# Split products over 272 tokens: operands of 288, 256 and 272 columns in place of three of 272

## The chip, the core and the metric

The kernel runs on one core of one Trainium2 chip. The metric is the device time of one execution in microseconds, as the median of several runs. Before the change it is 2591.55 us (three runs, 2590.3 to 2593.0).

## What is computed

A stack of blocks on 256 tokens with 2048 features, in float32. The first block puts 16 learned tokens (`meta`) ahead of the 256, so its products run over 272 tokens; the later ones run over 256.

```python
h = concatenate([meta, x])                        # 16 + 256 = 272 tokens
u = rms_norm(h, g_norm) @ w_in                    # hgrn2: q, f, i, z, each 2048 wide (products a_in, a_z)
...                                               # gates, chunked state, heads
h = h + (rms_norm(o) * silu(z)) @ w_out           # a_out
k, v, forget = rms_norm(h, g_kv) @ w_kv           # kv, and fl for the 16 forget columns
h = h + fox_mix(h, ...)                           # b_in, b_out: 256 tokens only
x = h[:, 16:]                                     # the 16 tokens are dropped
x = x + mixed(hyena(x), mlstm(x)) @ w_out         # w2, gates, mg, branches, out2
x = x + (silu(g) * u) @ w_down                    # gate_up, down
return rmsnorm(x)
```

## The kernel before, in words

Tokens lie along the free dimension and features along the 128 partitions, so a product is a set of matmuls whose stationary operand is a 128x128 tile of the weights and whose moving operand is a 128-feature tile of the input with all its tokens. To keep float32 accuracy with TensorE's fast float32 type, both are split: `hi` is the value rounded to the fast type, `lo` is the rest. One 128x128 tile of a product is therefore three matmuls into the same PSUM bank, in `passes` (lines 2007 to 2011): `w_hi` with `x_hi` (L2009), `w_hi` with `x_lo` (L2010), `w_lo` with `x_hi` (L2011). Such a set is called a triple here. `columns` (L2065) has the same three lines written out for the stages in which a product is spread between the work of heads (a_z over 272 tokens, b_in over 256): L2081 to L2083. `down_product` (L2126 to L2128) has the weights as moving operand, 512 columns wide.

Weights come in chunks of 128x1024 through a ring of 4 buffers (`raw`). The sync engine issues the transfers in the order of the chunks, each after VectorE is done with the buffer's last content. ScalarE writes `hi` from `raw` (`chunk`, L573, or `prep`, L578), VectorE writes `lo = raw - hi` (L1124, L1131), TensorE takes the chunk once `lo_ready` says so and frees it with `chunk_used`. The order of each engine's instructions is written out by hand: `follow` puts the work that follows a group of results behind the first few chunks of the next group.

`product` (L2013) goes over pairs; a pair has two groups `gg` of four output tiles (`j`), each group in four PSUM banks of its own (banks 0 to 3 or 4 to 7), over 16 input tiles `k`, two for each chunk. So a group is 16 x 4 x 3 = 192 matmuls. VectorE takes the four banks in one instruction: `scaled` (L1141 to 1148) multiplies by the reciprocal root mean square in `small` and releases the bank group with `bank_free`; `residual` (L1157 to 1162) adds to `H`. In a_z, `a_gate_out` (L1397 to 1402) takes one bank for each of 16 tiles. The work of the heads (lines 2150 to 2210 on TensorE, 1344 to 1389 on VectorE) stands between the parts of a_z.

The input's two halves lie in `XH` and `XL`, one after the other. For 272 tokens tile `k` starts at element 48 + 272k, for 256 tokens at 48 + 256k, with tile 0 at 32 (`STEP` is 16, `KICK` is 32, `WIDE` is 48). ScalarE writes the hi part of four tiles at a time (`a_piece`, `a_split`, `hi_part`), VectorE the lo part (`lo_part`, L1193; `first_x_lo`, L1253). For 272 tokens the two halves of a weight chunk in `hi` and `lo` are put 32 elements apart and shifted by 0 or 32 by the ring slot (`halves`, L356); for 256 tokens and in a_z they lie without gaps.

The products over 272 tokens are a_in (6 pairs), a_out (2), kv (4), each 384 matmuls a pair in triples, fl (16 triples) and a_z (256 triples).

## Time and profile before

| | |
|---|---|
| median of the runs | 2591.55 us (2590.3 to 2593.0) |
| span of the profiled execution | 2591.3 us |
| TensorE busy (matmuls) | 2564.5 us, 99% |
| VectorE busy | 1567.0 us, 60% |
| ScalarE busy | 1212.0 us, 47% |
| GpSimd busy | 69.1 us, 3% |
| DMA | 445.34 MB, 172 GB/s |
| granted TensorE clock, mean | 0.998 of full speed |

The profile is one execution. Engines are PE (TensorE's matmuls), PEld (its weight loads), DVE (VectorE), ACT (ScalarE), POOL (GpSimd). L2009 is line 2009 of the kernel. A matmul's duration in the profile is from its start to its modelled end and overlaps the next one, so the rate of TensorE is read from the distance between starts. The kernel goes, by time: a_in up to about 300 us, a_z with the heads up to 475 us, a_out up to 588 us, kv up to 756 us, fl up to 762 us, then the stages over 256 tokens, and from 2340 us down.

### The profile page before, as it was taken

What the parts mean: (1) busy time and instruction counts of PE and PEld (TensorE: products, weight loads), DVE (VectorE), ACT (ScalarE), POOL (GpSimd) and SP (SyncE); (2) the same over time, 40 slices, a digit from 0 to 9 for tenths busy, and PEclk for the clock granted to TensorE, in tenths of its full rate; (3) what the DMA queues carried; (4) which work ended last, traced back from release to release, by engine and by line L of the source; (5) the groups of instructions that cost most, each with busy time, mean ns of one, the idle gap of its engine ahead of it and who ended that gap; (6) DMA issues with size and microseconds to landing.
All of it is one profiled execution on the core that took longest, in us unless ns stands there. A gap on an engine that the chain in (4) does not pass through costs nothing.

```text
span 2591.3 us, 51017 instructions
## 1 busy us (share of the span) xinstructions
PE 2564.5 (99%) x20256; PEld 2475.2 (96%) x20256; DVE 1567.0 (60%) x1934; ACT 1212.0 (47%) x1432; POOL 69.1 (3%) x64
## 2 busy tenths in 40 slices
PE   9999999999999999999999999999999999999998
PEld 9999999999999999999999998789999999998887
DVE  6445677665456566577765556886655555555444
ACT  5344457543347765443445444334544444443343
POOL 0000022000000000000000000310000000000000
PEclk9999999999999999999999999999999999999999
DMA  6554532455554434655555654236565656566554
GB/s 230 179 175 166 165 112 90 141 173 184 174 173 167 139 123 147 195 196 192 190 193 179 203 194 131 82 107 202 184 199 190 193 193 192 190 193 207 191 187 154
DMA packets 122484, 445.34 MB, mean 172 GB/s; under 512 B 13787, under 2 KB 14070, under 8 KB 122225
## 3 DMA queue, kind: packets, MB, share of 16 engines
q1 hardware_dynamic: 121104, 438.75, 51.6%
q0 software_dynamic: 1248, 4.75, 0.5%
q8 instruction: 94, 1.54, 0.2%
q14 instruction: 38, 0.30, 0.0%
HBM read 441.35 MB, written 2.10 MB: 171 GB/s over the span
## 4 chain that ended last, share of the span: by engine, by line
PE 94%; DVE 3%; ACT 1%; issue 1%; DMA 0%; SPq 0%; DVEq 0%; ACTq 0%
PE PS L2011 23%; PE PS L2009 23%; PE PS L2010 23%; PE PS L2127 3%; PE PS L2126 3%; PE PS L2128 3%; PE PS L2081 3%; PE PS L2083 3%; PE PS L2082 3%; DVE lo L1131 1%; PE PS L2263 1%; PE PS L2454 1%; PE PS L2187 0%; PE PS L2203 0%; PE PS L2533 0%
## 5 line engine op out<-in xcount | busy, mean ns | idle before, releaser
L2009 PE MATMUL PS<-XH,hi 128*128 128x256 f32 (+1 forms) x5152 | 1448.1, 281 | 5.7 <-DVE lo L1124 2.2
L2011 PE MATMUL PS<-XH,lo 128*128 128x256 f32 (+1 forms) x5152 | 1444.3, 280 | 0.0
L2010 PE MATMUL PS<-XL,hi 128*128 128x256 f32 (+1 forms) x5152 | 1439.7, 279 | 0.0
L1124 DVE TENSOR_TENSOR lo<-raw,hi 128x1024 fp32r<-128x1024 f32 x703 | 851.8, 1223 | 757.0 <-ACT hi L573 753.7
L573 ACT ACTIVATE hi<-raw 128x1024 fp32r<-128x1024 f32 x703 | 739.9, 1059 | 949.9 <-PE PS L2011 800.1
L2009 PEld LDWEIGHTS PS<-XH,hi 128*128 128x128 f32 x5152 | 968.7, 188 | 9.0 <-DVE lo L1124 2.7
L2010 PEld LDWEIGHTS PS<-XL,hi 128*128 128x128 f32 x5152 | 971.0, 188 | 1.6 <-issue 1.4
L2011 PEld LDWEIGHTS PS<-XH,lo 128*128 128x128 f32 x5152 | 968.5, 188 | 0.0
L2081 PE MATMUL PS<-XH,hi 128*128 128x256 f32 (+1 forms) x768 | 225.8, 294 | 0.3 <-DVE XL L1196 0.3
L2083 PE MATMUL PS<-XH,lo 128*128 128x256 f32 (+1 forms) x768 | 216.8, 282 | 0.0
L1131 DVE TENSOR_TENSOR lo<-raw,hi 128x1024 fp32r<-128x1024 f32 x124 | 160.2, 1309 | 93.4 <-ACT hi L578 92.3
L2082 PE MATMUL PS<-XL,hi 128*128 128x256 f32 (+1 forms) x768 | 216.7, 282 | 0.0
L578 ACT ACTIVATE hi<-raw 128x1024 fp32r<-128x1024 f32 x124 | 129.0, 1051 | 106.7 <-PE PS L2011 75.6
L2081 PEld LDWEIGHTS PS<-XH,hi 128*128 128x128 f32 x768 | 145.2, 189 | 2.4 <-issue 1.4
L2082 PEld LDWEIGHTS PS<-XL,hi 128*128 128x128 f32 x768 | 145.4, 189 | 1.0
L2083 PEld LDWEIGHTS PS<-XH,lo 128*128 128x128 f32 x768 | 145.3, 189 | 0.0
L2126 PE MATMUL PS<-hi,GH 128*128 128x512 f32 x352 | 137.3, 390 | 0.0
L2127 PE MATMUL PS<-hi,GL 128*128 128x512 f32 x352 | 137.0, 389 | 0.0
L2128 PE MATMUL PS<-lo,GH 128*128 128x512 f32 x352 | 137.0, 389 | 0.0
L2128 PEld LDWEIGHTS PS<-lo,GH 128*128 128x128 f32 x352 | 66.1, 188 | 13.8
L2126 PEld LDWEIGHTS PS<-hi,GH 128*128 128x128 f32 x352 | 66.1, 188 | 13.7
L2127 PEld LDWEIGHTS PS<-hi,GL 128*128 128x128 f32 x352 | 66.1, 188 | 13.5
(357 smaller groups left out, 1557.8 us busy)
## 6 DMA issues: line engine op xcount, KB each, us to landing
raw<-stream SPq DMA_DIRECT2D x827, 512.0 KB, 4.2
out<-f_y SPq DMA_DIRECT2D x4, 512.0 KB, 3.1
H<-h_in SPq DMA_DIRECT2D x3, 544.0 KB, 6.7
w_t<-w POOLq DMA_DIRECT2D x2, 512.0 KB, 4.0
y_win<-windows POOLq DMA_DIRECT2D x2, 512.0 KB, 5.3
f_gain<-gain_f POOLq DMA_DIRECT2D x1, 1024.0 KB, 7.4
H<-h_in SPq DMA_DIRECT2D x2, 272.0 KB, 4.2
raw<-stream SPq DMA_DIRECT2D x2, 256.0 KB, 4.1
```

The costliest lines, as they stand in the source:

```text
L573: act.activation(halves(hi, s, q.tokens, q.shift), raw_halves(s), ACT.Copy).then_inc(hi_ready, 1)
L1124: dve.tensor_tensor(halves(lo, s, q.tokens, q.shift), raw_halves(s), halves(hi, s, q.tokens, q.shift).bitcast(F32), ALU.subtract)\
L1131: dve.tensor_tensor(halves(lo, k % RING, tokens_of(k)), raw_halves(k % RING), halves(hi, k % RING, tokens_of(k)).bitcast(F32), ALU.subtrac ...
L2009: pe.matmul(PS[:, bank, 0:n], w_hi, x_hi, start=start, stop=False)
L2010: pe.matmul(PS[:, bank, 0:n], w_hi, x_lo, start=False, stop=False)
L2011: return pe.matmul(PS[:, bank, 0:n], w_lo, x_hi, start=False, stop=stop)
L2081: pe.matmul(dst, hi[s][:, col], x_hi, start=k == 0, stop=False)
L2082: pe.matmul(dst, hi[s][:, col], x_lo, start=False, stop=False)
L2083: ins = pe.matmul(dst, lo[s][:, col], x_hi, start=False, stop=k == NT - 1)
L2126: pe.matmul(dst, x_hi, w_hi, start=False, stop=False)
L2127: pe.matmul(dst, x_lo, w_hi, start=False, stop=False)
L2128: ins = pe.matmul(dst, x_hi, w_lo, start=False, stop=k == FT - 1)
```

## The change

Only the products over 272 tokens change, and the layout that they need.

- The rest (`lo` part) of the first 16 tokens no longer lies at the head of the tile in `XL`. It is written behind the 272 rounded columns in `XH`, so that a tile of `XH` has 288 columns: 272 rounded ones and 16 rests. `XL` keeps the rests of the other 256 tokens alone.
- The triple becomes: `w_hi` with 288 columns of `XH` (the last 16 land in PSUM columns 272 to 287 of the bank), `w_hi` with 256 columns of `XL` (into PSUM columns 16 to 271), `w_lo` with 272 columns of `XH`.
- VectorE has to add PSUM columns 272 to 287 to the first 16: in `scaled` and `a_gate_out` with two more instructions (`meta_added`: multiply into a small buffer, add), in `residual` with one, for fl with two. The buffer's reuse is guarded by a wait for the other bank group's release, or for the gate before.
- Tiles of `XH` for 272 tokens have a pitch of 320 elements (`PITCH`), with tile 0 at 32 and the others at 48 + 320k, and tiles of `XL` have the place that the 256-token products use. Weight halves lie without gaps everywhere. The extra instructions that write the 16 rests stand in `lo_part` and `first_x_lo`; the hi part of the first piece is written in two instructions.
- `XH` grows and `XL` shrinks; some buffers of the later stages are moved in memory.

```diff
-        x_hi_flat = sb(ctx, "XH", [P, NT * T + 4 * STEP], F32R)
-        x_lo_flat = sb(ctx, "XL", [P, NT * T + 4 * STEP], F32R)
+        x_hi_flat = sb(ctx, "XH", [P, 2 * STEP + KICK + NT * PITCH], F32R)
+        x_lo_flat = sb(ctx, "XL", [P, 2 * STEP + KICK + NT * SEQ], F32R)
...
-            if tokens != T:
-                return buf[s][:, shift:shift + CHUNK].rearrange("p (h n) -> p h n", h=2)
-            at = 2 * STEP * (s % 2)
-            return buf[s][:, at:at + CHUNK + 2 * STEP].rearrange("p (h n) -> p h n", h=2)[:, :, 0:CHUNK // 2]
+        def halves(buf, s, shift=0):
+
+            return buf[s][:, shift:shift + CHUNK].rearrange("p (h n) -> p h n", h=2)
...
-            at = WIDE + k * T if n == T else KICK + (STEP + k * SEQ if k else 0)
+            at = KICK + (STEP + k * (SEQ if n == SEQ else PITCH) if k else 0)
             return flat[:, at:at + n]
...
+            def meta_added(n, dst, rest):
+
+                own(dve.tensor_tensor(meta_t[:, 0:n, :], rest, small[:, 1, 0:META].unsqueeze(1).to_broadcast([P, n, META]),
+                                      ALU.mult))
+                return dve.tensor_tensor(dst, dst, meta_t[:, 0:n, :], ALU.add)
+
             def scaled(q, dst, p_first):
...
+                    if q.tokens == T:
+                        own_last(ins)
+                        dve.wait_ge(bank_free[1 - gg], p + (q.use0[1 - gg] + 1 + gg))
+                        ins = meta_added(GROUP, at[:, :, 0:META], PS[:, 4 * gg:4 * gg + GROUP, T:T + META])
+                    ins.then_inc(bank_free[gg], 1)
...
+                if n == T:
+                    for part, tiles in x_parts(hi_flat, q, T + META):
+                        dve.tensor_tensor(part[:, :, T:], src[:, tiles, 0:META], part[:, :, 0:META].bitcast(F32), ALU.subtract)
+                for (dst, tiles), (part, _) in zip(x_parts(lo_flat, q, SEQ), x_parts(hi_flat, q, n)):
+                    ins = dve.tensor_tensor(dst, src[:, tiles, n - SEQ:], part[:, :, n - SEQ:].bitcast(F32), ALU.subtract)
...
-            def passes(bank, n, w_hi, w_lo, x_hi, x_lo, start, stop):
-
-                pe.matmul(PS[:, bank, 0:n], w_hi, x_hi, start=start, stop=False)
-                pe.matmul(PS[:, bank, 0:n], w_hi, x_lo, start=False, stop=False)
-                return pe.matmul(PS[:, bank, 0:n], w_lo, x_hi, start=False, stop=stop)
+            def passes(bank, col0, n, w_hi, w_lo, k, start, stop, xh=x_hi_flat, xl=x_lo_flat):
+
+
+
+                own = col0 + n - SEQ
+                wide = n + (META if n == T else 0)
+                pe.matmul(PS[:, bank, col0:col0 + wide], w_hi, x_tile(xh, k, wide), start=start, stop=False)
+                pe.matmul(PS[:, bank, own:col0 + n], w_hi, x_tile(xl, k, SEQ), start=False, stop=False)
+                return pe.matmul(PS[:, bank, col0:col0 + n], w_lo, x_tile(xh, k, n), start=False, stop=stop)
```

## Rows read from the trace of the kernel before

**Rows 1.** The page: busy time of the engines, granted clock, chain by engine.

```profile
PE 2564.5 (99%) x20256; PEld 2475.2 (96%) x20256; DVE 1567.0 (60%) x1934; ACT 1212.0 (47%) x1432; POOL 69.1 (3%) x64
...
PEclk9999999999999999999999999999999999999999
...
PE 94%; DVE 3%; ACT 1%; issue 1%; DMA 0%; SPq 0%; DVEq 0%; ACTq 0%
```

**Rows 2.** What PE waited for, largest row: us in total, times, longest.

```profile
PE PS L2009 <- DVE lo L1124: 2.2, 2, 1.8
```

**Rows 3.** Groups by line and form: count, then busy us, mean ns, idle before.

```profile
L2009 PE MATMUL PS<-XH,hi 128*128 128x256 f32 x3600 | 1000.4, 278 | 2.8 <-DVE MG L1863 1.9 <-DVEq L1701 0.6 <-DVE BZ L1522 0.4
...
L2009 PE MATMUL PS<-XH,hi 128*128 128x272 f32 x1552 | 447.6, 288 | 2.8 <-DVE lo L1124 2.2 <-DVE XL L1254 0.6
...
L2081 PE MATMUL PS<-XH,hi 128*128 128x272 f32 x256 | 79.0, 309 | 0.0
```

**Rows 4.** Timeline of PE in a_in: start us, us; 11 matmuls between.

```profile
100.13 0.29 PE L2009 MATMUL PS<-XH,hi 128*128 128x272 f32 x1
...
101.62 0.29 PE L2009 MATMUL PS<-XH,hi 128*128 128x272 f32 x1
```

**Rows 5.** Timeline of PE in gate_up, 256 columns; 11 matmuls between.

```profile
1884.83 0.28 PE L2010 MATMUL PS<-XL,hi 128*128 128x256 f32 x1
...
1886.19 0.28 PE L2010 MATMUL PS<-XL,hi 128*128 128x256 f32 x1
```

**Rows 6.** Timeline of PE in down, 512 columns; 11 matmuls between.

```profile
2349.91 0.39 PE L2126 MATMUL PS<-hi,GH 128*128 128x512 f32 x1
...
2352.63 0.39 PE L2126 MATMUL PS<-hi,GH 128*128 128x512 f32 x1
```

**Rows 7.** Timeline of PE in w2, 256 columns, slower stretch; 11 between.

```profile
1130.72 0.28 PE L2009 MATMUL PS<-XH,hi 128*128 128x256 f32 x1
...
1132.14 0.28 PE L2009 MATMUL PS<-XH,hi 128*128 128x256 f32 x1
```

**Rows 8.** Timeline of PE in a_z, 272 columns; 46 matmuls between.

```profile
313.96 0.29 PE L2082 MATMUL PS<-XL,hi 128*128 128x272 f32 x1
...
319.87 0.27 PE L2165 MATMUL PS<-cst,AV 128*16 128x128 f32 x1
```

**Rows 9.** Two lines of VectorE by source: ns min/median/max, first and last start.

```profile
L1350 DVE TENSOR_TENSOR a_W<-AB x16: 157/166/171, 308.6 to 451.3; 128x16 f32<-128x16 f32 x16
L1387 DVE COPY a_SS<-PS x16: 279/291/292, 329.4 to 469.9; 128x128 f32<-128x128 f32 x16
```

**Rows 10.** Timelines of DVE and PE around the first result of a_in.

```profile
41.74 1.29 DVE L1146 TENSOR_TENSOR AQ<-PS,small 128x1088 f32<-128x1088 f32 x1 [0.15 <-DVE a_VT L1307]
...
45.16 3.50 DVE L1124 TENSOR_TENSOR lo<-raw,hi 128x1024 fp32r<-128x1024 f32 x3 [2.13 <-ACT hi L573]
...
46.44 0.40 PE L2009 MATMUL PS<-XH,hi 128*128 128x272 f32 x1 [0.40 <-DVE lo L1124]
```

**Rows 11.** Timelines of DVE and PE from the last result of a_in on.

```profile
299.77 1.29 DVE L1146 TENSOR_TENSOR AV<-PS,small 128x1088 f32<-128x1088 f32 x1 [0.60 <-PE PS L2011]
...
310.41 0.44 DVE L1356 TENSOR_TENSOR a_W<-AQ,a_W 128x272 f32<-128x272 f32 x1 [1.68 <-ACT AB L698]
...
311.71 0.77 DVE L1402 TENSOR_TENSOR AZ<-PS,small 128x272 f32<-128x272 f32 x2
...
318.13 2.82 DVE L1131 TENSOR_TENSOR lo<-raw,hi 128x1024 fp32r<-128x1024 f32 x2 [2.55 <-ACT hi L578]
...
322.07 0.49 PE L2171 MATMUL PS<-cst,a_W 128*16 128x128 f32 x3 [1.71 <-DVE a_KT L1368]
```

**Rows 12.** Timeline of DVE in a running head.

```profile
344.97 0.42 DVE L1366 COPY a_KT<-PS 64x256 f32<-64x256 f32 x1 [1.72 <-PE PS L2171]
```

**Rows 13.** Timeline of DVE at the end of kv.

```profile
761.24 1.28 DVE L1146 TENSOR_TENSOR BV<-PS,small 128x1088 f32<-128x1088 f32 x1
763.16 2.43 DVE L1196 TENSOR_TENSOR XL<-BN,XH 128x256 fp32r<-128x256 f32 x3 [0.63 <-ACT XH L557]
```

More of the change, by code:

```diff
@@ L572, in chunk @@
                 act.wait_ge(chunk_used, q.index(p, gg, c) + 1)
-                act.activation(halves(hi, s, q.tokens, q.shift), raw_halves(s), ACT.Copy).then_inc(hi_ready, 1)
+                act.activation(halves(hi, s, q.shift), raw_halves(s), ACT.Copy).then_inc(hi_ready, 1)
             def prep(k):
@@ L1161, in after @@
                     dst = H[:, p * 8 + 4 * gg:p * 8 + 4 * gg + 4, T - q.tokens:T]
-                    dve.tensor_tensor(dst, dst, bank_group(gg, q.tokens), ALU.add).then_inc(bank_free[gg], 1)
+                    ins = dve.tensor_tensor(dst, dst, bank_group(gg, q.tokens), ALU.add)
+                    if q.tokens == T:
+                        own(ins)
+                        ins = dve.tensor_tensor(dst[:, :, 0:META], dst[:, :, 0:META],
+                                                PS[:, 4 * gg:4 * gg + GROUP, T:T + META], ALU.add)
+                    ins.then_inc(bank_free[gg], 1)
                     dve.wait_ge(bank_free[gg], p + (q.use0[gg] + 2))
@@ L1193, in lo_part @@
             def lo_part(lo_flat, hi_flat, q, n, src):
-                for (dst, tiles), (part, _) in zip(x_parts(lo_flat, q, n), x_parts(hi_flat, q, n)):
-                    ins = dve.tensor_tensor(dst, src[:, tiles, :], part.bitcast(F32), ALU.subtract)
+                if n == T:
[3 more added lines that the diff above has]
+                    ins = dve.tensor_tensor(dst, src[:, tiles, n - SEQ:], part[:, :, n - SEQ:].bitcast(F32), ALU.subtract)
                 return ins
@@ L1401, in a_gate_out @@
                     dve.wait_ge(S("a_vt"), tile - 3)
-                dve.tensor_tensor(a_gate(tile), PS[:, 1 + 2 * (tile % 2), 0:T], small[:, 1, 0:T], ALU.mult)\
-                    .then_inc(S("a_zout"), 1)
+                bank = 1 + 2 * (tile % 2)
+                own_last(dve.tensor_tensor(a_gate(tile), PS[:, bank, 0:T], small[:, 1, 0:T], ALU.mult))
+                if tile:
+                    dve.wait_ge(S("a_zout"), tile)
+                else:
+                    dve.wait_ge(bank_free[1], q.use0[1] + 1)
+                meta_added(1, a_gate(tile)[:, 0:META].unsqueeze(1), PS[:, bank:bank + 1, T:T + META]).then_inc(S("a_zout"), 1)
             def a_finish(g):
@@ L1492, in b_input @@
                 own(dve.tensor_tensor(F_row[:, 0, :], PS[0:HEADS, 0, 0:T], small[0:HEADS, 1, :], ALU.mult))
+                own(dve.tensor_tensor(F_row[:, 1, 0:META], PS[0:HEADS, 0, T:T + META], small[0:HEADS, 1, 0:META], ALU.mult))
+                own(dve.tensor_tensor(F_row[:, 0, 0:META], F_row[:, 0, 0:META], F_row[:, 1, 0:META], ALU.add))
                 dve.sem_inc(bank_free[0], 1)
@@ L2078, in columns @@
                     col = slice(128 * kk, 128 * kk + 128)
-                    dst = PS[:, bank, col0:col0 + q.tokens]
-                    x_hi, x_lo = x_tile(x_hi_flat, k, q.tokens), x_tile(x_lo_flat, k, q.tokens)
-                    pe.matmul(dst, hi[s][:, col], x_hi, start=k == 0, stop=False)
-                    pe.matmul(dst, hi[s][:, col], x_lo, start=False, stop=False)
-                    ins = pe.matmul(dst, lo[s][:, col], x_hi, start=False, stop=k == NT - 1)
+                    ins = passes(bank, col0, q.tokens, hi[s][:, col], lo[s][:, col], k, k == 0, k == NT - 1)
                 if kks.stop == 8:
```

85 lines of the change are left out of this document (42 added, 43 removed).

## Prediction

> **What bounds the kernel now.** I read the page's shares and its chain of work first [rows 1]: TensorE is busy for 2564.5 of 2591.3 us, and 94% of the chain that ended last is matmuls, nearly all at the three lines of the split product. So the time is the number of matmuls times the spacing between them, plus some 27 us in which TensorE stands idle; the waits of TensorE [rows 2] show no single stall longer than 1.8 us. The profiled span (2591.3 us) is 0.25 us below the median of the runs (2591.55 us), so what is worked out on the span can be set against the median.
>
> The second look is at the forms [rows 3]. There are 1552 triples of 272 columns at lines 2009 to 2011 (the products a_in, a_out, kv and the small fl), 256 more at lines 2081 to 2083 (a_z), together 1808; the later stages have triples of 256 columns, and down has 512 columns. The mean of one matmul in these rows is a latency with overlap, no price: the spacing of starts is, and it has to be taken from the timeline.
>
> Third look, the timeline. I count from a start to the twelfth start behind it. 272 columns in a product: 1.49 us, 124.1 ns each [rows 4]. 256 columns: 1.36 us, 113.3 ns [rows 5]. 512 columns: 2.72 us, 226.7 ns [rows 6]. The last two are in exact proportion, 0.4427 ns for a column. In that proportion 272 columns would take 120.4 ns, so each pays 3.7 ns more than its columns. That is not fixed to the width: in another stretch the same 256-column form runs at 1.42 us for twelve, 118.3 ns each, without a wait [rows 7], 5 ns above its columns; so there is a second way for these streams to run, and 256 can be in either. In a_z, where the weights lie unpadded and the input tile changes with every triple, 272 columns take 5.91 us for 47, 125.7 ns [rows 8]. The granted clock reads nine tenths or more in every slice [rows 1], so the engine stays at its 2.4 GHz level and the clock explains none of it.
>
> **The change, part by part.** *Columns.* Before, a triple streams 272 + 272 + 272 = 816 columns; after, 288 + 256 + 272 = 816. No column and no matmul is saved. A gain can come only from the 3.7 ns and 5.3 ns above proportion.
>
> *The triple in the products.* Price before: 3 x 124.1 = 372.3 ns. After, matmul by matmul: the 256-column one is taken at 113.3 ns [rows 5], with 118.3 ns as its upper end [rows 7]. The 272-column one stays at 124.1 ns. 288 columns in one matmul are nowhere in the trace; its columns cost 288 x 0.4427 = 127.5 ns, which is the lower end. For the upper end I let the excess grow with the columns above 256, twice 3.7, which gives 134.9 ns. I take 127.5 + 3.7 = 131.2, since 272 is the nearest width and 512, much wider, pays no excess at all [rows 6]. Sum 113.3 + 131.2 + 124.1 = 368.6 ns, 3.7 less than before. Times 1552: -5.7 us.
>
> *The triple in a_z.* Before 3 x 125.7 = 377.1 ns. The input tiles now start at a pitch of 320, a multiple of 64 elements, as the 256-column products have with their pitch of 256, and weights lie unpadded in both. I price it like the products, 368.6 ns: 8.5 x 256 = -2.2 us. If only the product's old pace is reached it is 4.8 x 256 = -1.2 us; if nothing, 0.
>
> A rule of the Trainium skill speaks against the change. In "TensorE: Matmul & The Clock Gate", section "Back-to-back issue gap", the warm spacing is the columns divided by 2.4 GHz plus 2.5 ns, which gives 109.2 ns for 256 and 115.8 ns for 272. The trace doesn't agree on the size. By that rule both triples cost the same 347.5 ns, and the change would bring nothing from TensorE. That outcome is the second rival below, worked out there from rows.
>
> *VectorE work added.* Each group result (scaled, 20 of them) gets two small operations on 4 x 16 elements, with a wait for the main one; each a_out group one; each of the 16 gates of a_z two; fl two; each input piece of 272 tokens one or two more for the rests. The nearest row is an operation on 128x16 at 167 ns, and a copy of 128x128 out of PSUM at 291 ns bounds it from above [rows 9]. I take 0.22 us for each dependent one, 0.45 us for a pair (0.3 to 0.6). In all some 90 operations, about 20 us on an engine that is busy for 1567 us; the main subtraction of the rests becomes 16 columns in 272 shorter. What counts is where TensorE waits for VectorE:
> - The first group result of a_in, at 41.7 us, is followed by ScalarE's Silu and weight rounding, VectorE's subtraction at 45.2 us, and a TensorE stall of 0.40 us at 46.4 us [rows 10]. Nothing covers the pair there: +0.45 us.
> - The last group result of a_in at 299.8 us is followed by the forget gates, scans, weight subtraction and the first two gates at 311.7 us, up to TensorE's stall of 1.7 us at 322.1 us [rows 11]. One pair, and two gates with a pair each: up to 1.3 us, of which a part falls into VectorE's own waits for ScalarE (1.7 and 2.6 us on the way). I take +0.9 us.
> - In the running heads the gate stands just ahead of the key copy, which at 345.0 us comes after 1.72 us of VectorE's waiting for TensorE; that hides the pair [rows 12]. Without that cover it would be 0.45 us x 12.
> - The last kv result at 761.2 us ends 0.63 us before the next subtraction can start, which waits for ScalarE [rows 13]: hidden. With a longer pair, up to 0.3 us.
> - The banks: TensorE comes back to a bank group one group later, 192 matmuls or 23.8 us, and the result now takes 1.75 instead of 1.3 us: hidden. The new wait for the other group's bank_free is for a result already written; behind it on VectorE only stand the small operations and the next subtractions, and it isn't due to last.
> - The two operations for fl and the extra cut of the first input piece: 0.1 us, between 0 and 0.4.
>
> Sum of these +1.4 us (0 to 3). DMA, and the masks and sums that are moved to other places in memory, cost nothing: the same number of transfers at the same places in the queues; that they would land on data in use is excluded by their old waits.
>
> **Sum.** -5.7 - 2.2 + 1.4 = -6.5 us: 2591.55 - 6.5 = 2585.0 us, 0.25% faster. Its own range from the terms' bounds is 2581 to 2589 us.
>
> **The rivals.**
> 1. *The excess vanishes in the whole triple.* For it: 256 and 512 run at exact proportion, and a 256-column matmul in every triple, with starts that always lie equally, may bring the stream back each time into the pattern of [rows 5]. Against it: [rows 7] shows that equal starts alone don't do that. Triple 816 x 0.4427 = 361.3 ns: -11.0 x 1552 = -17.1 us, -15.8 x 256 = -4.0 us, +1.4 us: 2571.8 us. In between, the excess of one more matmul gone, lies 2578 us.
> 2. *Only columns and their excess count.* The excess goes with the columns above 256: 16 + 16 + 16 before, 32 + 0 + 16 after, the same 48. Or it is an average over the places in a cycle that the streams run through either way. For it: the 124.1 ns doesn't change over the whole stage. Then products don't gain, a_z gains 0 to 1.2 us, VectorE's additions cost 1.4 us: 2591.8 to 2593 us, 2592 taken. (By the page's rule the same.)
> 3. *Slower.* The wide operand upsets the one behind it: the 256-column matmul runs at 118.3 ns [rows 7], and the 288-column one at 134.9 ns. Triple 118.3 + 134.9 + 124.1 = 377.3 ns, +5.0 x 1552 = +7.8 us, a_z 0, VectorE +1.4 us: 2600.8 us. It decides once a triple is above 372.3 ns + 2.5 ns. For it: the slow pattern of 256 columns follows a disturbance and then holds. Against it: 512-column matmuls stay clean next to their loads.
> That the change doesn't do what it says is small: the second operand has no other columns to stream.
>
> **Chances.** Forecast 0.32; rival 1 with its middle 0.30; rival 2 0.25; rival 3 0.13. 0.2%, 5.2 us, is about what a measurement of this kernel can tell from no change, so faster ends at 2586.4 us and slower begins at 2596.7 us. Of the forecast two thirds lie below 2586.4. Faster 0.22 + 0.30 = 0.52, same 0.10 + 0.25 = 0.35, slower 0.13. The range holds the forecast and rival 2, reaches to 2571 for nearly all of rival 1, and stops at 2597, short of rival 3 at its full price.
>
> **What would show it.** In the timeline of the changed kernel, in the stretch from 60 to 290 us: twelve matmuls in 1.474 us (four triples of 368.6 ns), and in them a step of 113.3 ns behind the 256-column start. 1.445 us would be rival 1, 1.49 us rival 2, 1.51 us rival 3. a_z should show the same triples as the products. The stall of 0.40 us near 46 us should read 0.8 to 0.9 us, the one near 322 us should be longer; the heads between should have none. The stages behind 770 us should have the same lengths as before. The prediction is wrong if the triples of 288, 256 and 272 have another sum, or if new waits for VectorE stand in the heads.

## The result, and the profile after

| | before | after |
|---|---|---|
| median, 20 runs each on one chip | 2591.47 us | 2596.28 us |
| ratio, with its 95% interval | | 1.0016 (1.0010 to 1.0022) |
| span of the profiled execution | 2591.3 us | 2594.2 us |
| device time of that execution | 2593.1 us | 2596.0 us |

The changed kernel is 4.8 us slower by the two medians and 4.1 us by the ratio (2.6 to 5.7 us), where 6.5 us less were forecast. So it moved the other way, clear of the noise. 2596.3 us lies at the upper end of the range, and with 0.16% just inside "within 0.2%". The last row corrects a sentence of the prediction: the device time is the span and 1.7 to 1.9 us more, in every run of a whole kernel here. So the profiled execution of before was no median one: it took 1.6 us more than the median, the one of after 0.3 us less. That is why the traces stand 2.9 us apart and the medians 4.8 us.

The page after, the same lines as [rows 1]:

```profile
PE 2565.2 (99%) x20256; PEld 2475.9 (95%) x20256; DVE 1583.2 (61%) x2029; ACT 1212.2 (47%) x1434; POOL 66.3 (3%) x64
...
PE 93%; DVE 4%; ACT 1%; issue 1%; DMA 0%; SPq 0%; DVEq 0%; ACTq 0%
```

The number of matmuls is the same; VectorE has 95 instructions and 16.2 us more, and one hundredth of the chain has passed from TensorE to it. All triples are at L2038 to L2040 now. Timeline of TensorE in a_in, columns as in [rows 4]: first four starts in a row, then the second matmul of a group, of its fourth input tile and of its last one, 36 and 144 matmuls apart.

```profile
102.43 0.30 PE L2038 MATMUL PS<-XH,hi 128*128 128x288 f32 x1
102.56 0.28 PE L2039 MATMUL PS<-XL,hi 128*128 128x256 f32 x1
102.68 0.29 PE L2040 MATMUL PS<-XH,lo 128*128 128x272 f32 x1
102.80 0.30 PE L2038 MATMUL PS<-XH,hi 128*128 128x288 f32 x1
```

```profile
85.35 0.28 PE L2039 MATMUL PS<-XL,hi 128*128 128x256 f32 x1
...
89.87 0.28 PE L2039 MATMUL PS<-XL,hi 128*128 128x256 f32 x1
...
107.79 0.28 PE L2039 MATMUL PS<-XL,hi 128*128 128x256 f32 x1
```

107.79 - 89.87 = 17.92 us for 48 triples, 373.3 ns each. The three tiles ahead of them took 4.52 us for 12 triples, 376.7 ns. Over whole groups that is 374.0 ns. In the same way before has 372.1 ns in every tile. Within a triple the steps average 133.1 ns behind the 288-column start, 116.6 ns behind the 256-column one and 124.3 ns behind the 272-column one. In a_z, from the second matmul of the first stretch to the head's work 47 matmuls later (the pair that answers to [rows 8]):

```profile
317.12 0.28 PE L2039 MATMUL PS<-XL,hi 128*128 128x256 f32 x1
...
322.72 0.28 PE L2039 MATMUL PS<-XL,hi 128*128 128x256 f32 x1
...
322.96 0.49 PE L2187 MATMUL PS<-cst,AV 128*16 128x128 f32 x3
```

5.84 us where before had 5.91. The widths differ here, so 5.84 us can't simply be divided by 47: the stretch holds 15 whole triples and then a 256-column and a 272-column step, and one of the dear 288-column steps is missing. The 15 whole triples, from 317.12 to 322.72 us, take 5.60 us, 373.3 ns each by these rounded rows. Over all of a_z at full clock, with the steps of each operand averaged, a triple takes 374.6 ns after 377.6. So a_z gained 3.0 ns, and the products lost 1.9 ns.

From the rates and the stalls below the whole difference can be added up: 1.9 x 1552 = +2.9 us, -3.0 x 256 = -0.8 us, and +2.3 us of stalls, together +4.4 us.

Where TensorE waits for VectorE, timeline of TensorE after, waits in brackets (they answer to [rows 10, 11]):

```profile
47.37 0.40 PE L2038 MATMUL PS<-XH,hi 128*128 128x288 f32 x1 [0.75 <-DVE lo L1120]
...
315.01 0.50 PE L2193 MATMUL PS<-cst,a_W 128*16 128x128 f32 x3 [0.83 <-POOL AB L511]
316.91 0.38 PE L2038 MATMUL PS<-XH,hi 128*128 128x288 f32 x1 [0.61 <-DVE lo L1127]
...
325.21 0.49 PE L2193 MATMUL PS<-cst,a_W 128*16 128x128 f32 x3 [1.76 <-DVE a_KT L1386]
...
334.42 0.68 PE L2220 MATMUL PS<-a_AM,a_VT 128*128 128x16 f32 x4 [0.46 <-DVE a_SS L1407]
...
432.01 0.72 PE L2232 MATMUL PS<-AF,cst 128*128 128x272 f32 x2 [1.01 <-ACT AQ L701]
```

Before, the same places read 0.40, 0.29, nothing, 1.71, nothing and 0.68 us. The four that grew and the two that are new come to 2.3 us. What VectorE does there (its timeline, the first group result and the first two gates):

```profile
42.27 1.29 DVE L1149 TENSOR_TENSOR AQ<-PS,small 128x1088 f32<-128x1088 f32 x1 [0.15 <-DVE a_VT L1325]
43.48 0.21 DVE L1139 TENSOR_TENSOR h_dif<-PS,small 128x64 f32<-128x64 f32 x1
43.73 0.23 DVE L1141 TENSOR_TENSOR AQ<-AQ,h_dif 128x64 f32<-128x64 f32 x1
...
314.26 0.43 DVE L1421 TENSOR_TENSOR AZ<-PS,small 128x272 f32<-128x272 f32 x1
314.61 0.16 DVE L1139 TENSOR_TENSOR h_dif<-PS,small 128x16 f32<-128x16 f32 x1
314.80 0.18 DVE L1141 TENSOR_TENSOR AZ<-AZ,h_dif 128x16 f32<-128x16 f32 x1
314.91 0.43 DVE L1421 TENSOR_TENSOR AZ<-PS,small 128x272 f32<-128x272 f32 x1
```

A pair at a group result ends 0.40 us after its main operation (43.96 against 43.56). At a gate the next one starts 0.65 us behind the last; before, two took 0.77 us together, 0.38 us each.

One thing in the two traces is not the change. Granted clock by stretch: behind the 1.7 us stall, before has a stretch at half speed, after none. First before, then after (stretch, length, TensorE busy, its granted clock, DMA share, GB/s):

```profile
324.00:326.00 2.00, 2.00 (x10) 0.50 0.64 201
326.00:328.00 2.00, 2.00 (x14) 0.75 0.55 217
```

```profile
326.00:328.00 2.00, 1.77 (x15) 1.00 0.78 248
328.00:332.00 4.00, 4.00 (x35) 1.00 0.42 135
```

At 0.50 of full speed, the 1.2 GHz level, the matmuls start 227 ns apart. Before's 24 matmuls from 323.83 us take 4.38 us to the last start, after's from 326.84 us 2.96 us: the change is credited 1.4 us there by chance. Of the runs below, three have such a drop too: the changed kernel without tile 0 set back (0.57 from 318 to 322 us, behind its stall at 317.8 us), the run at a pitch of 288 (behind its stall of 1.72 us at 320.5 us) and the run cut to 256 columns (from 294.7 us on). In the opening, from 12 to 20 us, the clock differs from trace to trace as well. Small differences have to be read from rates and stalls, or from medians, not from two spans.

### The profile page after: what moved, and what is told of

Read it like the earlier page. It is cut to its first block, busy times and chain, and to the rows that moved or that the text cites. A ratio compares the mean times of both kernels' runs of the same rounds, so it can differ in the third digit from the quotient of the medians.

```text
span 2594.2 us, 51114 instructions
## 1 busy us (share of the span) xinstructions
PE 2565.2 (99%) x20256; PEld 2475.9 (95%) x20256; DVE 1583.2 (61%) x2029; ACT 1212.2 (47%) x1434; POOL 66.3 (3%) x64
## 4 chain that ended last, share of the span: by engine, by line
PE 93%; DVE 4%; ACT 1%; issue 1%; DMA 0%; SPq 0%; DVEq 0%; ACTq 0%
PE PS L2038 26%; PE PS L2040 26%; PE PS L2039 25%; PE PS L2150 3%; PE PS L2149 3%; PE PS L2148 3%; DVE lo L1127 1%; PE PS L2285 1%; PE PS L2476 1%; PE PS L2209 0%; PE PS L2225 0%; PE PS L2554 0%; PE PS L2493 0%; PE PS L2220 0%; PE PS L2199 0%
## 5 line engine op out<-in xcount | busy, mean ns | idle before, releaser
L2038 PE MATMUL PS<-XH,hi 128*128 128x256 f32 (+1 forms) x5920 | 1688.5, 285 | 7.0 <-DVE lo L1120 3.2
L2040 PE MATMUL PS<-XH,lo 128*128 128x256 f32 (+1 forms) x5920 | 1657.9, 280 | 0.0
L2039 PE MATMUL PS<-XL,hi 128*128 128x256 f32 x5920 | 1645.2, 278 | 0.0
L2038 PEld LDWEIGHTS PS<-XH,hi 128*128 128x128 f32 x5920 | 1113.8, 188 | 12.3 <-DVE lo L1120 3.6
L2040 PEld LDWEIGHTS PS<-XH,lo 128*128 128x128 f32 x5920 | 1114.3, 188 | 0.0
L554 ACT ACTIVATE GH<-g_p 128x1024 f32 (+3 forms) x12 | 11.8, 990 | 46.9 <-DVE g_p L1986 46.9
L1058 ACT ACTIVATE g_s<-g_s 128x1024 f32<-128x1024 f32 x11 | 11.7, 1061 | 31.1 <-DVE g_s L1981 31.1
L510 POOL TENSOR_TENSOR a_W<-AF,a_W 128x272 f32<-128x272 f32 x16 | 14.1, 883 | 412.3 <-ACT AB L695 412.3
L692 ACT ACTIVATE a_W<-a_W 128x272 f32<-128x272 f32 x16 | 6.8, 427 | 38.1 <-DVE a_W L1368 38.0
L1211 DVE TENSOR_TENSOR GL<-g_p,GH 128x1024 f32 (+3 forms) x12 | 13.5, 1136 | 15.6 <-ACT GH L554 15.6
L2225 PE MATMUL PS<-AB,a_SS 128*128 128x64 f32 x128 | 17.8, 262 | 0.0
```

The source lines that it names most:

```text
L2038: pe.matmul(PS[:, bank, col0:col0 + wide], w_hi, x_tile(xh, k, wide), start=start, stop=False)
L2039: pe.matmul(PS[:, bank, own:col0 + n], w_hi, x_tile(xl, k, SEQ), start=False, stop=False)
L2040: return pe.matmul(PS[:, bank, col0:col0 + n], w_lo, x_tile(xh, k, n), start=False, stop=stop)
```

## The experiments

Two theories stood at the start. *Widths*: a 256-column matmul keeps its clean 113.3 ns only among its like, and 288 columns pay more above proportion than 272. *Places*: the loss comes from where the operands lie, since the change moved them all. The additions of VectorE got a run of their own. In all the rates below I count 144 starts (48 triples, tiles 3 to 15 of a group).

**A bare loop over widths.** The kernel keeps the streams and leaves out the computation. It runs triples of matmuls on constant operands, with the weights and input tiles where the products have them, in 24 sets one after the other. Its `passes`:

```diff
+                            for i, (wb, xb) in enumerate(((hi, x_hi_flat), (hi, x_lo_flat), (lo, x_hi_flat))):
+                                wd = widths[i]
+                                x = (xk + k * pitches[i]) if k else x0
+                                c0 = 16 if (wd == 256 and widths[0] > 256 and i == 1) else 0
+                                pe.matmul(PS[:, 4 * gg + j, c0:c0 + wd], wb[s][:, w], xb[:, x:x + wd], start=False, stop=k == groups[gg] - 1 and i == 2)
```

> The matmul stream by itself. It leaves out the whole computation and sends TensorE 24 sets of matmuls in the order of a product's group (16 input tiles, 4 output tiles, triples of w_hi x XH, w_hi x XL, w_lo x XH, weights in the ring's places) with static operands, each set behind eight 512-column matmuls and a short pause. Only widths, pitch and start of the input tiles and the gaps of the weights differ. Theory A (an excess that goes with the columns by which a width is no multiple of 64): 256 at 113.3 ns, 272 at 124.0, 288/256/272 at 373.9 ns a triple, 288 near 133, 304 at 138 to 141, and 320 back in proportion at 141.7 ns; 320/256/320 would take 396.7 ns. Theory B (the excess comes from where the reads start: input and weights in equal or opposite halves of 64 elements): 272 columns at the new pitch without gaps differ from the old places by over 1 ns, and sets that differ in the start alone (0, 16, 32, 48) differ at 256 columns too. Theory C (a matmul waits for the next weight load, slower the more the moving stream reads): the excess falls with the width, 384 columns at exactly 170.0 ns, and 240 and 128 columns stand at one floor near 112 ns. If 288/256/272 gives 373.9 ns here, the added 1.9 ns a triple of the changed kernel needs no other engine for its cause.

Measured per matmul, three equal widths: 128 columns 111.7 ns, 240: 112.2, 256: 117.8, 272: 124.4, 288: 132.6, 304: 140.0, 320: 145.6, 384: 173.3. A triple of 288, 256 and 272 takes 373.3 ns, 320, 256 and 320 410.0. So 320 columns, a multiple of 64, are not clean (141.7 ns in proportion): theory A, a rule by multiples of 64, falls. Of theory C the floor near 112 ns is there, but 384 columns stand 3.3 ns above its 170.0 ns. 256 never reached 113.3 ns here, though, with any start: something of the kernel's places was not met. `XL` happened to begin 32 elements off `XH`, counted in 64. At these places three of 272 columns take 373.3 ns too, as much as the new triple.

**The loop with XL in its true distance.** Same loop, `XL` a multiple of 64 elements behind `XH`, and sets that move starts.

```diff
-                                x = (xk + k * pitches[i]) if k else x0
+                                x = ((xk + k * pitches[i]) if k else x0) + (xladd if i == 1 else 0)
```

> The matmul stream by itself again (the computation is left out). In the first such run XL lay 32 elements off the real distance from XH modulo 64, and three times 256 columns ran at 117.8 ns and never at 113.3. Here the distance is a multiple of 64 as in both kernels, and sets are added in which XL's start is moved by 16, 32 and 48, the order of the three matmuls is changed, and tile 0 starts elsewhere. Theory B (the state that costs nothing needs equal starts of XH and XL modulo 64): the set of the 256-token products falls to 113.3 ns a matmul, the one with XL moved by 32 stays at 117.8, three times 272 at the old places gives 372.1 ns a triple, and 288/256/272 gives 373.9 ns and depends on XL's start by some ns. Theory D (the free state is a matter of how the stream was started, not of the starts of its operands): 256 stays at 117.8 ns in all sets, with tile 0 at 32 or at 48, and the triples of 816 columns all lie between 373 and 375 ns. If one of the added sets of 288/256/272 lies under 369 ns, it is the setting for a better kernel.

Now three of 256 columns run at 113.3 ns (340.0 ns a triple), but only where tile 0 starts at 32 or 0 and the others at 48. With tile 0 at 48 too, the stream stays at 117.8 ns; timeline of TensorE, tiles 3 to 15 of that set:

```profile
81.08 0.28 PE L350 MATMUL PS<-XH,hi 128*128 128x256 f32 x1
...
98.04 0.28 PE L350 MATMUL PS<-XH,hi 128*128 128x256 f32 x1
```

16.96 us for 144. With all tiles at 0 it is 120.0 ns, and with `XL` moved by 32 elements 117.8 ns. The two paces are those of [rows 5, 7], and in the loop, with the other tiles at 48, the shift of tile 0 decides between them. In the kernel before, the stretch of [rows 7] has that shift too, and the same product runs at 113.3 ns from 1145 us on; what put it into the slower pace stays open. A single wider neighbour is enough: 256, 256 and 272 columns take 357.8 ns, where 113.3 + 113.3 + 124.1 would be 350.7. 288, 256 and 272 columns take 373.3 ns with tile 0 set back or not, and with the three in another order. 3 x 272 at the changed kernel's places takes 370.0 ns: less than the new triple.

**Every place in the real distance.** A third loop with the true gaps between weight halves, and starts that vary.

```diff
-                        at = (32 * (s % 2) + kk * 544) if pad else kk * 512
+                            at = (kk * 512, 32 * (s % 2) + kk * 528, kk * 544)[pad]
```

> The matmul stream by itself (the computation is left out), the sets now with the kernel before's true weight places (half pitch 528, odd slots 32 further) and with the a_z order (one output tile at a time, all input tiles). The last such run gave 353.3 ns for 3 x 256 where the input starts elsewhere than 48 past the weights (modulo 64) or where the first tile isn't set back by 16, 373.3 ns for 288/256/272 and 370.0 ns for 3 x 272 in the changed kernel's places. Theory E (the distance of input and weights modulo 64 sets the pace, and the widths add theirs): the kernel before's places give 372.1 ns in every input tile; 3 x 272 at a pitch of 288 with the weight halves 32 apart, which keeps that distance, gives 370.0 ns like the pitch of 320; with the halves unpadded 373 to 379 ns; other starts (0, 16, 32) 373 to 380 ns. The a_z order gives about 377 ns at the old places, 373.3 ns for 288/256/272 and 370 ns for 3 x 272 at pitch 320. Theory F (only the shape of the triple counts, 370.0 was a chance state of one start): the sets of 3 x 272 scatter between 370 and 379 ns without regard to the distance, and moving tile 0 from 32 to 48 loses the 370.0.

Timelines of TensorE, tiles 3 to 15. First 3 x 256, then before's own triple and places, then 3 x 272 at a pitch of 320, then the new triple, then 3 x 288:

```profile
33.50 0.28 PE L344 MATMUL PS<-XH,hi 128*128 128x256 f32 x1
...
49.82 0.28 PE L344 MATMUL PS<-XH,hi 128*128 128x256 f32 x1
```

```profile
63.67 0.29 PE L344 MATMUL PS<-XH,hi 128*128 128x272 f32 x1
...
81.53 0.29 PE L344 MATMUL PS<-XH,hi 128*128 128x272 f32 x1
```

```profile
196.01 0.28 PE L344 MATMUL PS<-XH,hi 128*128 128x272 f32 x1
...
213.78 0.28 PE L344 MATMUL PS<-XH,hi 128*128 128x272 f32 x1
```

```profile
538.73 0.30 PE L344 MATMUL PS<-XH,hi 128*128 128x288 f32 x1
...
556.65 0.30 PE L344 MATMUL PS<-XH,hi 128*128 128x288 f32 x1
```

```profile
869.28 0.29 PE L344 MATMUL PS<-XH,hi 128*128 128x288 f32 x1
...
888.48 0.29 PE L344 MATMUL PS<-XH,hi 128*128 128x288 f32 x1
```

16.32, 17.86, 17.76, 17.92 and 19.20 us: 340.0, 372.1, 370.0, 373.3 and 400.0 ns a triple. The loop gives both kernels' real rates in the products to a tenth. Moving all tiles of the 370.0 ns case from 48 to 0, 16 or 32 gives 376.0, 380.0 and 380.0 ns, and moving `XL` alone 373.3 ns. In a_z's order of tiles, before's places give 378.3 ns, the new triple 373.6 and 3 x 272 at a pitch of 320 370.0; the kernels have 377.6 and 374.6 ns for the first two, so the loop is within 1 ns there. Widths and places both count, with opposite signs in the changed kernel: places gain 2.1 ns a triple (8 in a_z), widths lose 3.3 ns (3.6 in a_z).

The two aren't independent, though. The second and third loop together have both triples at seven settings of the starts:

| tiles at, `XL` moved by | 3 x 272, ns | 288, 256, 272, ns |
|---|---|---|
| 48, 0 (the changed kernel) | 370.0 | 373.3 |
| 0, 0 | 376.0 | 376.7 |
| 16, 0 | 380.0 | 373.3 |
| 32, 0 | 380.0 | 380.0 |
| 48, 16 | 373.3 | 377.8 |
| 48, 32 | 373.3 | 373.3 |
| 48, 48 | 373.3 | 377.8 |

With the tiles at 16 the new widths are the cheaper ones. Timelines of TensorE, tiles 3 to 15, first 3 x 272 in the third loop, then the new triple in the second, 18.24 and 17.91 us:

```profile
260.79 0.29 PE L344 MATMUL PS<-XH,hi 128*128 128x272 f32 x1
...
279.03 0.29 PE L344 MATMUL PS<-XH,hi 128*128 128x272 f32 x1
```

```profile
561.50 0.29 PE L350 MATMUL PS<-XH,hi 128*128 128x288 f32 x1
...
579.41 0.29 PE L350 MATMUL PS<-XH,hi 128*128 128x288 f32 x1
```

So "widths lose 3.3 ns" is their price at the changed kernel's places; at the others they cost between -6.7 and +4.4 ns. The new widths at before's own places have no run.

**The changed kernel cut to 256 columns.** Behind the first input tile of each group the two matmuls with `XH` are cut to 256 columns, which leaves out the last 16 tokens and the rests of the first 16. If the changed kernel's places or its traffic kept the clean pace away, it would stay away here too.

```diff
+                if n == T and not start:
+                    pe.matmul(PS[:, bank, col0:col0 + SEQ], w_hi, x_tile(xh, k, n)[:, 0:SEQ], start=start, stop=False)
+                    pe.matmul(PS[:, bank, own:col0 + n], w_hi, x_tile(xl, k, SEQ), start=False, stop=False)
+                    return pe.matmul(PS[:, bank, col0:col0 + SEQ], w_lo, x_tile(xh, k, n)[:, 0:SEQ], start=False, stop=stop)
```

> The changed kernel with the 272-token triples cut to 256/256/256 columns behind the first input tile of each group: the last 16 tokens are left out of the two products with XH and the rests of the first 16 are left out. Layout, VectorE work and order stay. It asks whether the new layout can carry the clean pace at all while ScalarE and VectorE write weights. If the loss comes from the widths (288 and 272 never meet the clean state), the triples run at 340.0 ns behind the first tile, the products over 272 tokens lose 33.9 ns for each of 1695 triples, some 57 us, and the kernel takes about 2539 us. If the layout itself (pitch 320, weights without gaps) keeps the stream in the slower state, the triples run at 353.3 ns, and it takes about 2561 us.

2546.74 us, against 2593.0 of before beside it, one execution of each. That is 46.3 us less, between the two expected times. The mean gain is smaller than 33.9 ns a triple, because each group's first tile still takes 380.7 ns, parts of a_z run at up to 353.7 ns, and TensorE now stalls for weights in some places (0.28 us at 220.6, 243.1 and 265.6 us). Timeline of TensorE in the same group of a_in:

```profile
83.61 0.28 PE L2040 MATMUL PS<-XL,hi 128*128 128x256 f32 x1
...
99.92 0.28 PE L2040 MATMUL PS<-XL,hi 128*128 128x256 f32 x1
```

16.3 us for 48 triples, 340 ns. With ScalarE and VectorE writing and the DMA running, the places allow the clean pace right behind the first tiles. So the widths 288 and 272 keep it away. The same rows settle another point. In the new triple the 256-column matmul writes to PSUM columns 16 to 271, not to column 0 on. It still does so here, at 340 ns a triple, so that offset isn't what costs; and in the third loop 272, 288 and 256 columns, all written from column 0, take 373.3 ns too.

**Without the additions.** The changed kernel without VectorE's extra work on results. It leaves out the additions in `scaled`, `residual`, the gates of a_z and fl, so the rests of the first 16 tokens are computed and not added.

```diff
-                    if q.tokens == T:
-                        own_last(ins)
-                        dve.wait_ge(bank_free[1 - gg], p + (q.use0[1 - gg] + 1 + gg))
-                        ins = meta_added(GROUP, at[:, :, 0:META], PS[:, 4 * gg:4 * gg + GROUP, T:T + META])
...
```

> The changed kernel without the additions of PSUM columns 272 to 287: meta_added in scaled and in the gates of a_z, the one in residual, and the two for fl are left out, with the wait for the other bank group, so the rests of the first 16 tokens are computed and not added. If the loss is that of the triples alone (1.9 ns x 1536, and a kick at each group's start), VectorE's additions are worth little: this kernel is 0.5 to 1 us faster than the changed one, some 2595.5 us where the changed one has 2596.3 and the kernel before 2591.5. If the additions carry the loss (rival: chains at the stage ends), it comes out within 1 us of the kernel before. In the profile the stall at 47 us should fall from 0.75 to 0.40 us, and the stall at 315 us from 0.83 to 0.29 us.

2594.87 us, 1.0009 of before (1.0000 to 1.0019). The rate is that of the changed kernel (374.0 ns). Two of the three stalls are back at before's length, the middle one not quite (before 0.29 us):

```profile
46.51 0.40 PE L2023 MATMUL PS<-XH,hi 128*128 128x288 f32 x1 [0.36 <-DVE lo L1120]
...
313.78 0.50 PE L2178 MATMUL PS<-cst,a_W 128*16 128x128 f32 x3 [0.46 <-POOL AB L511]
...
429.31 0.72 PE L2217 MATMUL PS<-AF,cst 128*128 128x272 f32 x2 [0.72 <-ACT AQ L701]
```

0.36, 0.46 and 0.72 us in place of 0.75, 0.83 and 1.01, and those at 316.91 and 334.42 us are gone: 2.1 us. That is more than the 0.5 to 1 us expected. By the ratios the additions cost 0.07%, 1.8 us, but with 2.9 us to either side that alone doesn't show a cost: the stalls do.

**Before's triple at a pitch of 288.** It computes everything. The weight halves lie 32 elements apart in all ring slots. It was meant as a half of the places' gain that fits into memory easily.

```diff
+PITCH = 288
-            at = WIDE + k * T if n == T else KICK + (STEP + k * SEQ if k else 0)
+            at = KICK + (STEP + k * (SEQ if n == SEQ else PITCH) if k else 0)
...
```

> The kernel before with its triple of 272/272/272 and without the additions, in places that fit the memory and keep the distance of input and weights at 48 modulo 64: input tiles at a pitch of 288 with tile 0 at 32, weight halves 32 elements apart in all ring slots. It does the layout part of the change alone. Theory E: triples at 370.0 ns in the products, 2.1 less than before's 372.1, less 11 ns for four triples at each group's first tile: 1536 x 2.1 = 3.2 us less, 24 groups x 44 ns = 1.1 us more, a_z between its old 377 and 373 ns (0 to 1 us less): 2.1 to 3.1 us below the kernel before, and 6 to 8 us below the changed one. Theory F: triples at 372 to 375 ns, no better than the kernel before (0 to +3 us). No stall should be longer than before's, since VectorE has the old work but one more instruction's cut of the first piece.

2592.62 us, 1.0002 (0.9993 to 1.0011). The 370.0 ns that were expected aren't there: the steady triple is 371.7 ns, as in the third loop (371.7), and the first tiles take 373.2 and 376.2 ns, so the mean is 372.1 as before: no gain. Tile 0 set back costs here, and 3 x 272 columns get nothing for it.

**The widths alone, in the whole kernel.** The kernel without the additions, with three times 272 columns again at the same places. Its second operand reads 272 columns of `XL` that belong to other tokens, and the rests of the first 16 tokens aren't read, so it leaves out part of the rests. One start differs: tile 0 of `XL` lies at 48, not at 32.

```diff
+                if n == T:
+                    pe.matmul(PS[:, bank, col0:col0 + n], w_hi, x_tile(xh, k, n), start=start, stop=False)
+                    at = STEP + KICK + ((k - (k % 4 == 3)) if k >= 4 else k // 2) * SEQ
+                    rest = xl[:, at:at + T]
+                    pe.matmul(PS[:, bank, col0:col0 + n], w_hi, rest, start=False, stop=False)
+                    return pe.matmul(PS[:, bank, col0:col0 + n], w_lo, x_tile(xh, k, n), start=False, stop=stop)
...
```

> The changed kernel's places (pitch 320, tile 0 at 32, weight halves without gaps), none of its additions, and 272, 272, 272 columns in a triple again. It leaves out the rests of the values: the second operand of a triple reads 272 columns in XL from a start that is as far from the weights and from XH as in the changed kernel, but their values belong to other tokens, and the first one has no 16 rests. So against the kernel without the additions it differs in widths alone. My theory (the widths 288 and 256 cost more than three of 272 at the same places): triples of 370.0 ns behind the first input tile, about 371 ns on the mean, in a_z too, 3 ns less than 373.97 ns, so 1808 x 3 = 5.4 us less than without the additions: 0.999 of the kernel before (0.998 to 1.000). Rival (the widths don't matter, the loss is the new places): 374 ns again, and 1.001 of the kernel before.

2587.28 us, 0.9982 (0.9973 to 0.9991). Triples of 370.0 ns behind the first tiles, 370.4 on the mean. Timeline of TensorE in a_in (second matmul, fourth tile, last tile):

```profile
83.66 0.29 PE L2028 MATMUL PS<-XL,hi 128*128 128x272 f32 x1
...
88.12 0.29 PE L2028 MATMUL PS<-XL,hi 128*128 128x272 f32 x1
...
105.88 0.29 PE L2028 MATMUL PS<-XL,hi 128*128 128x272 f32 x1
```

Against the run without the additions the widths differ (and that one start), and 1.0009 - 0.9982 = 0.27%, 7.0 us, with 3.4 us to either side. From the rates: (374.0 - 370.4) x 1552 = 5.6 us, and 374.3 - 371.2 ns in a_z, 0.8 us. The widths of the change are its loss.

**Tile 0 like the others.** The same with tile 0 of the 272-token products at 48, and then the whole changed kernel so.

```diff
-            at = KICK + (STEP + k * (SEQ if n == SEQ else PITCH) if k else 0)
+            at = KICK + (STEP + k * (SEQ if n == SEQ else PITCH) if k or meta else 0)
...
```

> As the run with 272, 272, 272 columns at the changed kernel's places, with the same parts left out, but tile 0 of a product over 272 tokens starts at 48 like the others, not at 32. My theory: tile 0 set back costs about 10 ns a triple for its four triples in each group and buys nothing at these widths. Then the triples are 370.0 ns from the first tile on, 24 groups x 40 ns = 1 us less than with it, 0.9985 of the kernel before. Rival (the set-back tile is what brings the stream to its better pace): triples stay at 373 ns or more without it, and the time is longer than with it.

2588.03 us, 0.9983 (0.9974 to 0.9992): 370.0 ns from the first triple on, but no gain that the medians show.

> The changed kernel whole, additions too, but tile 0 of the products over 272 tokens starts at 48 in XH and XL, not at 32. Nothing is left out. My theory: the pace of 373.3 ns is there from the first tile, and 380 and 376.8 ns of the first two input tiles are gone: 1.0 us less than the changed kernel, a ratio of 1.0012 to 1.0014 against the kernel before where the changed kernel had 1.0016. Rival (tile 0 set back is needed at these widths, as it is for 256 columns, where without it a matmul takes 117.8 and not 113.3 ns): the triple is above 373.3 ns all through, up to 377 ns, and the ratio is 1.003 or more.

2594.99 us, 1.0011 (1.0002 to 1.0020). Timeline of TensorE, group's start and fourth tile:

```profile
86.59 0.28 PE L2039 MATMUL PS<-XL,hi 128*128 128x256 f32 x1
...
91.08 0.28 PE L2039 MATMUL PS<-XL,hi 128*128 128x256 f32 x1
```

36 matmuls in 4.49 us after 4.52 us, that is 374.2 ns a triple in place of 376.7 by rounded rows; over nine groups it is 373.3 ns in all tiles. The rates give 1.0 us (373.96 - 373.33, times 1552), the ratios 0.05%, 1.3 us, with intervals that overlap. The set-back tile isn't needed at these widths.

**The places alone, with nothing left out.** It computes everything, as the kernel before does. Both input halves at a pitch of 320 need 4 KB more of each partition than in the changed kernel. They fit if the tail of `XL` shares its room with a buffer of the second block that is written later, and three buffers of the first block lie in `h2_sum` and `h2_dif`.

```diff
+        with ExitStack() as ph:
+            x_lo_flat = sb(ph, "XL", [P, 2 * STEP + KICK + NT * PITCH], F32R)
+        sb(ctx, "XL_256", [P, 2 * STEP + KICK + NT * SEQ], F32R)
...
+            sb(ph, "XL_tail", [P, 960])
             AQ = sb(ph, "AQ", [P, NT, T])
...
+            a_AM = [sb(ph, "a_AM0", [P, T]), h2[:, 0:T]]
...
+            b_PT = [sb(ph, f"b_PT{s}", [P, 640]) for s in range(2)]
             BK = sb(ph, "BK", [P, NT, T])
...
```

> The kernel before with the changed kernel's places alone: three matmuls of 272 columns with all their values, no additions, XH and XL both at a pitch of 320 with tile 0 at 32, weight halves without gaps. The room for the longer XL comes from b_PT, which now lies over its tail in the second block, and from a_AM, gam and dec, which lie in h2_sum and h2_dif in the first. Nothing is left out. My theory (the places are the half of the change that gains, the widths the half that loses): triples of 370.0 ns behind the first input tile, 370.4 on the mean, in a_z 371 after 376.8: 1552 x 1.7 + 256 x 5.8 = 4.1 us less than before, 0.9984 of it (0.9975 to 0.9993). Rival (the 0.9982 with the rests left out came from something that the missing values or XL's shorter tiles bring): triples of 372 ns and a ratio of 1.000.

2588.66 us, 0.9985 (0.9976 to 0.9994): 370.0 ns behind the first tiles, 370.6 on the mean, 371.4 in a_z. The rates give (372.1 - 370.6) x 1552 + (377.6 - 371.4) x 256 = 3.9 us, as the ratio does.

> As the run with 272 columns three times at a pitch of 320 and nothing left out, but tile 0 starts at 48 like the others. My theory: 370.0 ns in every triple of the products from the first on, 24 groups x 40 ns = 1.0 us less than with tile 0 at 32: 0.998 of the kernel before. Rival (tile 0 set back makes no difference between two whole runs): the same ratio within 0.0003, and only the trace shows the 380 ns triples gone.

2587.45 us, 0.9981 (0.9972 to 0.9990), the fastest kernel here that computes everything: 4.6 us less than before. The two can't be told apart by their medians. Timeline of TensorE in the group of a_in (second matmul, fourth tile, last tile):

```profile
84.87 0.28 PE L2013 MATMUL PS<-XL,hi 128*128 128x272 f32 x1
...
89.31 0.28 PE L2013 MATMUL PS<-XL,hi 128*128 128x272 f32 x1
...
107.07 0.28 PE L2013 MATMUL PS<-XL,hi 128*128 128x272 f32 x1
```

4.44 us and 17.76 us, 370.0 ns in both. The rates account for (372.1 - 370.0) x 1552 = 3.3 us in the products, and its a_z for the rest: 370.6 ns a triple after 377.6 (from 313.37 to 319.17 us 47 equal matmuls, 370.2 ns a triple, where [rows 8] has 377.1), 7.0 x 256 = 1.8 us; together 5.1 us.

## Why the prediction was wrong

- *What bounds the kernel.* Right: all of the result is in the spacing of matmuls and in TensorE's stalls for VectorE. The step that set the span beside the median was wrong by 1.8 us, without effect on the forecast. The range "from the terms' bounds", 2581 to 2589 us, doesn't follow from them: with 127.5 ns for 288 columns and no stalls the sum is 2577 us, with 118.3 and 134.9 ns, nothing in a_z and 3 us of stalls it is 2602 us.
- *The triple in the products: the step that failed.* Forecast 113.3 + 131.2 + 124.1 = 368.6 ns, measured 116.6 + 133.1 + 124.3 = 374.0 ns. The difference of 5.4 ns is 8.4 us of 1552 triples, most of the 11.3 us between forecast and result; a_z has 1.4 us of it and the stalls 0.9 us. Two terms failed, by 3.3 and 1.9 ns: the 256-column price was taken from a stage in which every matmul is that wide [rows 5], and the 288-column one was given the excess of its neighbour of 272. The loops have 113.3 ns only where the whole stream is 256 columns wide, with its starts in certain places (240 columns reached it too). It is no price of a matmul: a single one among wider ones took 116.1 ns or more in the loops' steady stretches at the changed kernel's places. The excess above proportion is 5.1 to 5.8 ns at 288, with 3.7 at 272 [rows 4].
- *Columns aren't the price.* Both triples have 816 columns, 361.3 ns by proportion. By the formula of the Trainium skill ("TensorE: Matmul & The Clock Gate", section "Back-to-back issue gap"), which the page gives for a matmul by itself and not for a stream with weight loads, they cost the same. The loop has 370.0 and 373.3 ns for them at the changed kernel's places, and 380.0 and 373.3 ns with the tiles at 16: the measurement decides, and what widths cost depends on the places.
- *a_z.* Forecast -8.5 ns a triple with -4.8 as the bound, measured -3.0 ns: -0.8 us, not -2.2, which is short of the bound too. With 3 x 272 the same places give -6.2 ns (-8 in the loop), and the widths take half of it back. The forecast had it right that the places matter here, and priced the products' places at nothing, where they are worth 2.1 ns.
- *VectorE.* Forecast +1.4 us, measured 1.8 by the ratios (not clear of noise) and 2.1 to 2.3 by stalls, inside 0 to 3. The pair was sized right (0.40 us against 0.45). At 46 us +0.35 for +0.45, and from 300 to 322 us +1.2 for +0.9. The heads were the miss: the pair is hidden in most of them, but at 334.42 and 432.01 us 0.46 and 0.33 us come through. The end of kv is hidden, as forecast.
- *What was not in the sum.* The set-back tile 0 comes with the new layout. Before had none in the 272-token products. It costs 1.0 us by the rates.
- *The rivals.* Rival 3 had the mechanism: the wide operand and the one behind it are both dearer (133.1 and 116.6 for its 134.9 and 118.3). But its triple of 377.3 ns was 3.3 ns too dear, 5.1 us, and its own threshold, 2.5 ns above 372.3, wasn't reached. Rival 2's claim that excess goes with columns above 256 fails by 3.3 ns at equal places. It came near in the products only because the places gained meanwhile. Rival 1's 361.3 ns is excluded.
- *The signs.* Twelve starts take 1.49 us in the changed kernel (17.92 us for 144), the sign that was set for rival 2, though the widths had changed the triple. The sign of the prediction being wrong, new waits in the heads, came true at 334.42 us.

The sum as measured, from the ratios: places -3.9 us (tile 0 set back among it), widths +7.0 us, additions +1.8 us: +4.9 us, where the two kernels directly have +4.1 us by the ratio and +4.8 us by the medians. Each term has an interval of 2 to 3.5 us to either side, and widths and additions are differences along one chain of runs that ends in the changed kernel, so the agreement confirms only the places. The rates and stalls, which don't rest on the medians, give +4.4 us. So the failed step and the loss are shown. Why the widths upset the stream, whether by the weight load beside it or by the reads of the input, no run here shows.

## What to carry to other kernels

The distance between the starts of two matmuls was here a property of the stream it is in, its neighbours' widths and all start addresses included. Price a changed stream from rows of the same mixture, or measure it in a bare loop first: here the loop gave the real rates of both kernels' products to 0.1 ns a triple, once its places were the real ones. The first loop, with one buffer 32 elements off, had no difference between the two triples. When a change moves widths and places at once, run each alone: one half of this one was worth having, and it didn't need the other. And the price of one half holds only at the other's setting: the same widths cost 3.3 ns at one start and saved 6.7 ns at another.

## What was not expected of the hardware

- Narrower hardly helped below 256 columns with these float32 operands: 128 columns take 111.7 ns, 240 take 112.2 to 113.3, 256 take 113.3, 117.8 or 120.0 by their starts.
- Starts matter. All that were compared are multiples of 16 elements, and equal ones modulo 64 agree at pitches of 256 and 320 (340.0 ns for 3 x 256 in both); finer steps weren't run. With weights without gaps and `XL` a multiple of 64 behind `XH`, three of 272 columns take 370.0 ns with all tiles at 48, and 376.0 to 380.0 ns at 0, 16 or 32.
- The clean pace of 256 columns had to be started in the loop: tile 0 at another place (32 or 0) and the rest at 48 gives 340.0 ns a triple from the third tile on, all at 48 stays at 353.3 ns. For the 272-column stream the same shift costs two tiles at more than 370.0 ns (378.5 and 371.0 ns in the kernel at a pitch of 320) and brings nothing.
- Behind a stall of 1.7 us the granted clock read 0.50 and then 0.75 of full speed in one trace and 1.00 in another: 1.4 us by chance, as much as a term of the sum. Four of the ten traces of whole kernels have such a drop near the start of a_z.
